# Tile order on VectorE and TensorE at the start of a two-layer streaming encoder

## The reference

```python
for layer in range(DEPTH):                      # DEPTH = 2
    h = rmsnorm(x, norm_w[layer])
    if layer % 2 == 0:
        proj = h @ ev_w_in[i]                   # 1024 x 2304
        u, g_a, q, k, v, g_b = split_cols(proj, ...)
        a_out = s5_mixer(u, ...) * silu(g_a)    # 32 groups of 64 complex diagonal states
        b_out = swa_mixer(q, k, v, sinks, rel_bias) * silu(g_b)
        mix = concatenate([a_out, b_out]) @ ev_w_out[i]
    else:
        proj = h @ od_w_in[i]
        c_out = gla_mixer(q, k, v, a_lr, ...) * silu(r)
        mix = c_out @ od_w_out[i]
    x = x + mix
return rmsnorm(x, final_norm)

def rmsnorm(x, w):
    return x * rsqrt(mean(x * x, axis=-1) + EPS) * w
```

## Time and profile before

| | us |
|---|---|
| median of 3 runs | 1696.81 |
| lowest and highest | 1696.63, 1697.51 |
| profiled execution, its time | 1697.39 |
| profiled execution, its span | 1695.6 |
| PE busy in the span | 1642.8 (97%) |
| DVE busy | 822.4 (49%) |
| ACT busy | 631.0 (37%) |
| POOL busy | 277.8 (16%) |

### The profile page before, as it was taken

The page is one execution under the profiler, slowest core; times in us unless marked ns, Lnnn a source line. Parts: engine busy times, 40 slices in busy tenths (PEclk is TensorE's granted clock), DMA queues, the critical chain, the costliest instruction groups (busy, mean ns, idle before and its releaser), DMA issues.

```text
span 1695.6 us, 22567 instructions
## 1 busy us (share of the span) xinstructions
PE 1642.8 (97%) x7898; PEld 1332.0 (79%) x7898; DVE 822.4 (49%) x1655; ACT 631.0 (37%) x1584; POOL 277.8 (16%) x500
## 2 busy tenths in 40 slices
PE   6999999999999799999999999999999999999997
PEld 4777788777777578888778888888888888878886
DVE  6744545667666473543552334333334443254443
ACT  6522334666666472332461222222222232131121
POOL 3883000000000431200000122212221221000000
PEclk9999999999999899999999999999999999999999
DMA  5466544454444946222242333333323332276663
GB/s 215 145 180 187 152 152 134 143 167 140 139 149 127 276 108 240 100 82 93 78 155 98 114 109 115 113 103 109 128 96 101 128 103 81 94 240 190 191 189 109
DMA packets 222216, 236.18 MB, mean 139 GB/s; under 512 B 53112, under 2 KB 169496, under 8 KB 222104
## 3 DMA queue, kind: packets, MB, share of 16 engines
q1 hardware_dynamic: 221528, 233.59, 43.5%
q10 hardware_dynamic: 576, 1.15, 0.2%
HBM read 140.12 MB, written 94.57 MB: 138 GB/s over the span
## 4 chain that ended last, share of the span: by engine, by line
PE 61%; DVE 2%; ACT 1%; DMA 1%; issue 0%; SPq 0%; POOLq 0%; POOL 0%; DVEq 0%; ACTq 0%
PE odd_bank L2143 29%; PE odd_bank L2298 10%; PE odd_bank L2189 10%; PE odd_bank L2168 2%; PE odd_bank L2248 2%; PE odd_bank L2245 2%; PE odd_bank L2246 2%; PE odd_bank L2227 1%; PE odd_bank L2152 1%; PE odd_bank L2203 1%; DMA scr_heads<-odd_ga_min 1%; PE odd_bank L2229 0%; PE odd_bank L2256 0%; PE odd_bank L2230 0%; PE odd_bank L2255 0%
## 5 line engine op out<-in xcount | busy, mean ns | idle before, releaser
L2143 PE MATMUL odd_bank<-ht_hi,odd_w_hi 128*128 128x512 f32 x768 | 318.4, 415 | 0.0
L2143 PE MATMUL odd_bank<-ht_lo,odd_w_hi 128*128 128x512 f32 x768 | 300.6, 391 | 0.0
L2143 PE MATMUL odd_bank<-ht_hi,odd_w_lo 128*128 128x512 f32 x768 | 298.8, 389 | 0.0
L1214 PE MATMUL ev_acc<-ht_hi,ev_w_hi 128*128 128x512 f32 x576 | 239.6, 416 | 2.3 <-DVE ht_lo L926 2.3
L1214 PE MATMUL ev_acc<-ht_hi,ev_w_lo 128*128 128x512 f32 x576 | 226.6, 393 | 0.0
L1214 PE MATMUL ev_acc<-ht_lo,ev_w_hi 128*128 128x512 f32 x576 | 226.3, 393 | 0.0
L1919 DVE COPY odd_stage<-odd_bank 128x512 f32<-128x512 f32 x96 | 66.3, 691 | 224.7 <-PE odd_bank L2143 224.7
L2143 PEld LDWEIGHTS odd_bank<-ht_lo,odd_w_hi 128*128 128x128 f32 x768 | 144.1, 188 | 31.8
L2143 PEld LDWEIGHTS odd_bank<-ht_hi,odd_w_hi 128*128 128x128 f32 x768 | 144.4, 188 | 29.9 <-issue 3.0
L2143 PEld LDWEIGHTS odd_bank<-ht_hi,odd_w_lo 128*128 128x128 f32 x768 | 144.6, 188 | 27.7
L1214 PEld LDWEIGHTS ev_acc<-ht_hi,ev_w_hi 128*128 128x128 f32 x576 | 108.7, 189 | 30.8 <-issue 5.5
(11 more groups left out here) (284 smaller groups left out, 2877.2 us busy)
## 6 DMA issues: line engine op xcount, KB each, us to landing
odd_gl_in<-scr_heads SPq DMA_DIRECT2D x32, 640.0 KB, 4.3
scr_heads<-odd_stage SPq DMA_DIRECT2D x64, 256.0 KB, 2.2
odd_w_raw<-od_w_in SPq DMA_DIRECT2D x24, 512.0 KB, 3.9
ev_w_raw<-ev_w_in SPq DMA_DIRECT2D x17, 512.0 KB, 6.5
ev_s_cos_sin<-scr_s_cos_sin SPq DMA_DIRECT2D x32, 256.0 KB
odd_xo_sum<-x SPq DMA_DIRECT2D x16, 512.0 KB, 4.1
scr_x<-odd_xo_sum SPq DMA_DIRECT2D x16, 512.0 KB, 2.9
scr_gla_mix<-odd_gl_out SPq DMA_DIRECT2D x32, 256.0 KB, 2.1
```

Of the source, the lines that this page charges most:

```text
L1214: mm = pe.matmul(acc[n % 3][:], w[j][:, k, :], h[:, k, t], start=(k == 0 and r == 0), stop=(k == KT - 1 and r == 2))
L2143: mm = pe.matmul(acc[n % 4][:], w[j][:, k, :], h[:, k, t], start=(k == 0 and q == 0), stop=(k == KT - 1 and q == 2))
```

## The change

The change reorders instructions on four engines; nothing is added or removed.

- VectorE: the clamp moves from ahead of the loop to behind tile 3's low part. For tiles 0 to 3 no set-up piece stands between the tiles. `normed(4)` moves from behind `lower(2)` to behind `lower(3)`, followed by the second weight tile's low part, the clamp, `normed(5)`, and the second piece. The third piece stands behind `normed(6)`. Every later piece stands two tiles later than before.
- TensorE: four turns instead of five stand ahead of half product 0. Turn 4 comes behind it, directly ahead of turn 5.
- ScalarE: the exponentials move from behind tile 2 to behind tile 4, the sines with their two table loads from behind tile 4 to behind tile 5. The three parameter DMAs stay behind tile 5 and now follow the sines.
- GpSimd: the first piece of `turns` moves from behind `inverse(5)` to behind `inverse(6)`.

```diff
@@ gpsimd
                 for t in range(NT):
                     inverse(t)
-                    if t >= 5:
+                    if t >= 6:
                         next(rest, None)
@@ scalar
                     upper(t)
                     if t == 0:
                         exp_group_step()
-                    if t == 2:
+                    if t == 4:
                         exp_decay()
                     if t == 3:
                         split(1)
-                    if t == 4:
+                    if t == 5:
                         sines()
-                    if t == 5:
                         load_bc()
@@ vector
                 normed(0)
                 split(0)
                 normed(1)
-                next(rest)
                 for t in range(NT):
                     lower(t)
                     if t == 3:
+                        normed(4)
                         split(1)
-                    if t + 2 < NT:
+                        next(rest)
+                    if t != 2 and t + 2 < NT:
                         normed(t + 2)
-                    if t >= 1:
+                    if t >= 3:
                         next(rest, None)
@@ tensor
-                for t in range(5):
+                for t in range(4):
                     turn_x(t)
                 for p in range(p_end):
...
+                    if p == 0:
+                        turn_x(4)
                     if p + 5 < NT:
                         turn_x(p + 5)
```

## The result

| | before | changed |
|---|---|---|
| median, us | 1696.76 (4 runs, 1696.63 to 1697.51) | 1705.18 (4 runs, 1703.62 to 1706.0) |
| profiled execution, time and span | 1697.39, 1695.6 | 1706.0, 1704.2 |
| ratio, 95% interval | | 1.0046 [1.0034, 1.0057] |
| measured again (experiment 5) | 1696.48 (24 runs, 1694.85 to 1700.85) | 1702.26 (6 runs, 1699.91 to 1704.36), 1.0032 [1.002, 1.0045] |

The forecast was 1699.2 with a range up to 1702.0, and "within 0.2%" was held likeliest. The median is 8.4 us above that of before, 5.8 in the repetition. The ratio is worked out from all runs and isn't the quotient of the two medians.

What follows compares the result with a forecast made beforehand. TensorE, busy 97%, bounds the kernel, its first stage a chain over four engines. Lag 1.2 at half product 8 grows to 2.4 at 12: 1697.39 + 2.4 = 1699.8 profiled, 1699.2 against the median; range 1695.6 to 1702.0.

Steps and rivals of the forecast that it cites:

- within 0.2%: Whole kernel: time the same as before within what a measurement can tell, 0.2% or 3.4 us; chance 66%.
- First product, 22.9: TensorE's first product, freed by VectorE's earlier low part of tile 3, starts at 22.9, 3.75 us early.
- Half product 1, 30.1: TensorE, after 12 slow products and turns 4 and 5: starts at 30.1 instead of 33.04, lead 2.95 us.
- Turn 6 after a wait of 0.85: TensorE waits 0.85 us for normed(6) and starts turn 6 at 33.8, lead 2.1 us.
- Turn 7, the angles, the sines, the square: Range reduction behind normed(6): angles 35.5, square 7 at 37.3, turn 7 at 40.8 after 3.35 us wait, lag 1.3.
- Rival A: ScalarE's DMA issues stand behind the table load: square 7 at 38.6, lag 3.7 us, 1700.5 us; chance 22%.
- The drain: ScalarE table switch: skill's extra of about 1.38 us would bring square 7 up to 1.4 later, 1700.6 us.
- Half product 8 at 62.3, half product 12 at 77.2: TensorE's later first stage: lag 1.2 us at half product 8, 2.4 us at half product 12.
- VectorE's term (a + b in, e out): VectorE before half product 12: pieces a to d replace c to e, 1.6 us more, of which 0.4 was slack.
- rival B: TensorE's clock falls at turn 7's gap, next 12 products 2.4 us slower: lag 4.8, 1701.6 us; chance 14%.
- The rest: nothing: Behind the first stage: GpSimd's turn factors some 3 us later, taken up by its 4.95 us wait; first powers cost nothing.
- rival D: Lag taken up later: up to 1.5 of TensorE's 2.5 us of waits shrink, giving 1697.7 us; chance 14%.

Runs made afterwards that it cites:

- experiment 5: The changed kernel again, unedited; 1702.26 us (6 runs), ratio 1.0032 [1.002, 1.0045].
- experiment 3: Kernel before with TensorE's part of the change alone: four turns ahead of the first product, turn 4 behind half product 0; 1703.12 us, ratio 1.0038.
- experiment 10: Kernel before with GpSimd's first turn piece three tiles later, behind the inverse of tile 8 instead of 5; 1696.68 us, ratio 0.9994.
- experiment 2: Changed kernel with spare products in TensorE's gaps, 12 ahead of turn 7 and 10 ahead of half product 8; 1700.41 us, ratio 1.0024.
- experiment 6: Changed kernel with spare products in four gaps: 12 ahead of turn 7, 10 ahead of half product 8, eight in each odd-layer gap; 1702.11 us, ratio 1.0027.
- experiment 1: Changed kernel with the end of the range reduction ahead of normed(6) instead of behind it; 1699.63 us, ratio 1.0014.
- 8: Kernel of experiment 4 with the first powers ahead of normed(8), so later set-up pieces stand one tile earlier; 1696.59 us, ratio 1.0002.
- 4: Kernel of experiment 1 with both sines, table loads and DMAs behind tile 7's square, GpSimd's first piece one tile later; 1698.16 us, ratio 1.0005.

## Why the prediction was wrong

The steps, in the prediction's order:

- **First product, 22.9.** Measured 22.98. Right, and experiment 3 shows the condition it rests on, VectorE's new order.
- **Half product 1, 30.1.** Measured 29.07. The failed assumption is that the clock rises at the same age of the run of products as before. Of the first products 12 were slow before; over the twelve profiles it is 6 to 12, and 9 in experiment 10, whose TensorE has the order of before. One execution could not show this spread. Here it was worth 1.1 us; between the profiles it is worth up to 1.4 (7.33 us from the first product to half product 1 in experiment 2, 5.92 in experiment 6).
- **Turn 6 after a wait of 0.85.** 32.70 after 0.64. Right, shifted by the clock.
- **Turn 7, the angles, the sines, the square.** Forecast relative to turn 6: angles +1.7, square 7 +3.5, turn 7 +7.0. Measured: 34.39, 36.16 and 39.65, that is +1.7, +3.5 and +6.95. The wait was forecast as 3.35 and was 3.11. This chain was right to a quarter of a microsecond, and experiment 1 shows that it hangs on the place of the range reduction.
- **Rival A** is refuted: the issues ran beside the load, as the copy in the earlier trace rows had suggested. The drain of the Trainium skill's "ScalarE: Activation LUTs" (section "What ACT_TABLE_LOAD costs") doesn't show here either: the square starts 0.01 us behind the load's end.
- **Half product 8 at 62.3, half product 12 at 77.2.** Measured 63.32 and 79.36; with the clock held 62.81 and 77.26. VectorE's term (a + b in, e out) was right.
- **The clock, rival B at 14%, is the step that failed in the stage.** The forecast put the cost of slower products behind turn 7 at nothing. They came in both executions of the changed kernel, at turn 7, and a second time at half product 8, which no rival had. Rival B priced one fall at 2.4 us, 12 slow products. The measured one is 5.29 - 3.64 = 1.65, because the clock was back after some six products; the second is 4.45 - 2.86 = 1.59. The sum of the stage: 2.4, less 1.4 for the early rise of the clock (54.47 us from the first product to half product 12 in experiment 2, 53.10 in experiment 6), plus 3.3 for two falls, is 4.3; measured 4.5. The rule of the Trainium skill's "TensorE: Matmul & The Clock Gate" (Part 1, an idle engine falls back to the lower clock; Part 4, transposes do not engage the higher one) spoke against the forecast. The trace agrees with Part 1 at turn 7: 36.55 to 40.93 without a product, one turn of two halves in it, and 0.77 and 0.63 behind. Whether the turn counts for nothing, as Part 4 has it, no run here shows; the clock was already falling while it ran. I had the rule and the row of 1.91 us without a fall, which said nothing of a gap of 4.2, and gave B too small a chance.
- **"The rest: nothing"**, and rival D's giving back, are wrong for the changed kernel. 1.2 us were added at the wait for the taps in both executions. The lag behind that grew by 2.7 us more in one execution and shrank by 1.1 in the other. In the first, the wait at the layer change added 0.7, the slow products behind it 0.5 and the fall at an odd gap 1.6; in the other they took 0.1 and 0.7 off and added nothing. What is left, up to 0.3 us, has no name. The wait at the layer change was 10.3 to 13.4 us in the twelve profiles, and why it varies no run shows. GpSimd's own wait did shrink, from 4.95 to 2.86, and TensorE got nothing of it. I had VectorE "less loaded" there and didn't ask what runs beside it; by the SBUF rule above a later VectorE meets GpSimd's train at another point, for better or worse.

With the early rise, the two falls and the taps the forecast of 1699.2 becomes 1699.2 - 1.4 + 3.3 + 1.2 = 1702.3. The repetition's median is 1702.26. That the two are so near is luck: the terms are read from single profiles, the repetition's six runs lie 4.5 us apart, the repetition's profile had another -1.1 us behind the taps, and filling the gaps, which takes the 3.3 away, left the median where it was. The first median, 1705.18, is 2.9 above the repetition's, the intervals of the two ratios overlap, and this difference stays open.

## What to carry to other kernels

An earlier start is kept only where the next late piece isn't moved behind it: the same reordering that freed the first product put the range reduction, the sines and the square of tile 7 in one line in front of turn 7. A stall of the matrix engine should be priced twice, once as the wait and once as the slower work behind it, and where no row of the kernel shows a gap of that size without a fall, the fall is to be reckoned with; spare products in the gap hold the clock. And a lead of 1 to 2 us at the start of a kernel whose executions differ by 5 us is not worth a rearrangement of four engines.

## What the runs showed of the hardware

- The clock's fall is no fixed function of a gap. Behind 1.9 us it fell in some executions and not in others: at 6 of 18 odd gaps in nine profiles (twice in those of experiments 3 and 8, once in that of 4 and in the first of the changed kernel, never in that of the kernel before). Behind the wait of 2.44 us at half product 8 it fell in both executions of the changed kernel and not in experiment 1. A fall cost 1.6 to 1.7 us, less than the 5.26 - 2.87 = 2.4 us of 12 slow products at the very start. At both gaps of the stage the granted clock stayed at 1.00 through the wait and fell once TensorE had begun again.
- After the first product the clock rose behind 6 to 12 slow products, differently in executions with the same order there; behind the wait at the layer change it rose behind 13 and 7 in the two executions of the changed kernel.
- ScalarE issues DMAs while a table is loading or a function runs: the three issues from 34.49 to 35.78 cost the square behind them nothing.
